# mLSTM numerators turned around, heads finished one by one, and the gate product moved ahead of the merge gates

## The reference, cut to what matters

```
proj = hn @ w_in                       # conv inputs, v, o, 16 gate columns, merge gates
s = einsum('bhcjd,bhcsd->bhcjs', qc, kc) * exp(dlog - m_j[..., None])
num = einsum('bhcjs,bhcsv->bhcjv', s, vc) + ...
den = sum(s, axis=-1) + ...
h = num / maximum(abs(den), exp(-m_j))[..., None]
y_b = o * (h_fwd + h_bwd)
mixed = sigmoid(merge_a) * (y_a @ w_branch_a) + sigmoid(merge_b) * (y_b @ w_branch_b)
```

## Time and profile before

| | |
|---|---|
| median of 3 runs | 2682.91 us (2682.42 to 2683.18) |
| the profiled execution | 2683.47 us, its span 2681.7 us |
| granted TensorE clock, mean | 0.993 of full |
| TensorE busy | 2626.6 us, 98% |
| VectorE busy | 1575.3 us, 59% |
| ScalarE busy | 1201.5 us, 45% |
| share of DMA engines' time | 50.2% for the weights |
| the load of a window, issue to landing | 5.9 us |

### The profile page before, as it was taken

How to read it: one execution, slowest core, us unless ns; L and a number is a source line. 1 busy time by engine, 2 the same in 40 slices (tenths; PEclk the granted TensorE clock), 3 DMA queues, 4 the chain that set the end, 5 groups by cost and what they waited for, 6 DMA issues and landing times.

```text
span 2681.7 us, 53183 instructions
## 1 busy us (share of the span) xinstructions
PE 2626.6 (98%) x21374; PEld 2541.4 (95%) x21374; DVE 1575.3 (59%) x1909; ACT 1201.5 (45%) x1402; POOL 43.1 (2%) x48
## 2 busy tenths in 40 slices
PE   8999999999999999999999988999999999999997
PEld 8999999999999989999999984679999999999997
DVE  6445778565465566777755454666565555555554
ACT  5444466443357654534444452124444444444432
POOL 0000121000000000000000000000000000000000
PEclk9999999999999999999999998999999999999999
DMA  6555532555545435656565550215655556565564
GB/s 223 178 175 169 168 102 80 165 177 175 178 159 171 134 103 165 198 191 197 194 202 193 191 180 16 71 63 188 194 191 190 188 188 199 185 202 195 191 193 130
DMA packets 123699, 445.95 MB, mean 166 GB/s; under 512 B 13594, under 2 KB 15925, under 8 KB 123440
## 3 DMA queue, kind: packets, MB, share of 16 engines
q1 hardware_dynamic: 122208, 438.82, 50.2%
q0 software_dynamic: 1360, 5.27, 0.6%
HBM read 441.94 MB, written 2.10 MB: 166 GB/s over the span
## 4 chain that ended last, share of the span: by engine, by line
PE 91%; DVE 4%; ACT 3%; issue 1%; DMA 0%; POOL 0%; DVEq 0%; SPq 0%; ACTq 0%
PE PS L1801 25%; PE PS L1799 25%; PE PS L1800 25%; PE PS L1862 2%; PE PS L1864 2%; PE PS L1863 2%; PE PS L2198 2%; PE PS L2266 1%; DVE lo L1025 1%; PE PS L2187 1%; ACT hi L530 1%; PE PS L1946 0%; PE PS L2209 0%; PE PS L1962 0%; PE PS L2045 0%
## 5 line engine op out<-in xcount | busy, mean ns | idle before, releaser
L1799 PE MATMUL PS<-XH,hi 128*128 128x256 f32 (+1 forms) x5152 | 1449.6, 281 | 15.7 <-DVE lo L1019 11.6
L1801 PE MATMUL PS<-XH,lo 128*128 128x256 f32 (+1 forms) x5152 | 1444.5, 280 | 0.0
L1800 PE MATMUL PS<-XL,hi 128*128 128x256 f32 (+1 forms) x5152 | 1440.0, 280 | 0.0
L1019 DVE TENSOR_TENSOR lo<-raw,hi 128x1024 fp32r<-128x1024 f32 x704 | 853.4, 1224 | 759.6 <-ACT hi L525 756.3
L525 ACT ACTIVATE hi<-raw 128x1024 fp32r<-128x1024 f32 x704 | 740.4, 1059 | 954.8 <-PE PS L1801 932.9
L1799 PEld LDWEIGHTS PS<-XH,hi 128*128 128x128 f32 x5152 | 969.6, 188 | 20.9 <-issue 19.2
L1800 PEld LDWEIGHTS PS<-XL,hi 128*128 128x128 f32 x5152 | 971.7, 189 | 2.3 <-issue 2.2
L1801 PEld LDWEIGHTS PS<-XH,lo 128*128 128x128 f32 x5152 | 969.2, 188 | 0.0
L1862 PE MATMUL PS<-XH,hi 128*128 128x256 f32 (+1 forms) x768 | 229.4, 299 | 0.3 <-DVE XL L1090 0.3
L1864 PE MATMUL PS<-XH,lo 128*128 128x256 f32 (+1 forms) x768 | 216.2, 282 | 0.0
L1863 PE MATMUL PS<-XL,hi 128*128 128x256 f32 (+1 forms) x768 | 216.0, 281 | 0.0
(11 more groups left out here) (327 smaller groups left out, 1598.9 us busy)
## 6 DMA issues: line engine op xcount, KB each, us to landing
raw<-stream SPq DMA_DIRECT2D x828, 512.0 KB, 4.1
H<-h_in SPq DMA_DIRECT2D x4, 544.0 KB, 8.3
y_win<-windows POOLq DMA_DIRECT2D x2, 1024.0 KB, 5.9
out<-H SPq DMA_DIRECT2D x4, 512.0 KB, 3.8
dftm<-dft POOLq DMA_DIRECT2D x1, 1024.0 KB, 5.9
w_t<-w POOLq DMA_DIRECT2D x2, 512.0 KB, 7.8
ml_m<-mask_ml POOLq DMA_DIRECT2D x1, 512.0 KB, 3.9
a_m<-masks_a POOLq DMA_DIRECT2D x1, 272.0 KB, 6.5
```

The lines of the kernel that those rows point to most:

```text
L1019: dve.tensor_tensor(halves(lo, s, q.tokens), raw_halves(s), halves(hi, s, q.tokens).bitcast(F32), ALU.subtract)\
L1799: pe.matmul(PS[:, bank, 0:n], w_hi, x_hi, start=start, stop=False)
L1800: pe.matmul(PS[:, bank, 0:n], w_hi, x_lo, start=False, stop=False)
L1801: return pe.matmul(PS[:, bank, 0:n], w_lo, x_hi, start=False, stop=stop)
```

## The change

Three things are changed together, with their places in SBUF.

1. **Order of the products.** `w2` is cut to 7 rounds. The mini product of the gates follows it, and then the merge gates as a product of their own, `mg`, of 4 rounds. The gate rows are made in between the chunks of `mg`'s first group; the extracts of both engines' lists are below. The stream of weights is in the new order.
2. **Numerators.** The weighted scores are now the stationary operand, the values the moving one, with a 257th column of ones. A numerator has the target tokens on partitions and its divisor in the last column. The matmuls of L2180 and L2280 are gone.
3. **Each head alone.** After each n VectorE makes two inverses for each partition (`divisors`); ScalarE scales the forward numerator (`forward`), VectorE scales the backward one and adds (`both_ways`), TensorE transposes the sum back (`m_turn`), and VectorE gates it (`mlstm_output`). The last head's end lies inside the first Hyena unit.

Beside these, the window buffer is one instead of two, its loads and that of the Fourier matrices are issued at other times, filter tiles of unit 0 go to banks 0, 1, 4 and 5, and the 16 `br_b` columns stand in other places: 0 and 1 before the first input spectrum, then (2, 3), (5, 6), (8, 9) and (11, 12, 13) ahead of the way back, (4), (7), (10) and (14, 15) behind it.

```
-    p["w2"] = Product(11, 8, 0, SEQ)
+    p["w2"] = Product(7, 8, 0, SEQ)
     p["gates"] = Mini(0, SEQ)
+    p["mg"] = Product(4, 8, 0, SEQ)
...
+            q = prod["mg"]                                       # ScalarE
+            tail_mg = follow(act, q, chunk, lambda: None, [(4, through(q, MG, 0, ACT.Sigmoid, "merge_gates"))],
+                             early={2: tail_w2, 4: gate_rows, 6: gate_logs}, nth=5)
...
+            q = prod["mg"]                                       # VectorE
+            tail_mg = follow(dve, q, chunk, lambda: None, [(4, scaled(q, MG, 0))],
+                             early={2: tail_w2, 3: mlstm_gates, 5: gate_sizes, 6: gate_sums, 7: gate_maxima})
...
+                def divisors(n):
+                    h, d = n // 2, n % 2
+                    dve.wait_ge(S("m_num"), n + 1)
+                    if n == 0:
+                        dve.wait_ge(S("m_c"), 2)
+                    r = m_R[:, n, :]
+                    den = PS[:, 4 + 2 * d:6 + 2 * d, 2 * P]
+                    own(dve.tensor_copy(r, den))
+                    own(dve.scalar_tensor_tensor(out=r, in0=r, scalar=-1.0, in1=r, op0=ALU.mult, op1=ALU.max))
+                    own(dve.tensor_tensor(r, r, m_F[:, 8 * d + h:8 * d + h + 5:4], ALU.max))
+                    own(dve.reciprocal(r, r), "m_r", n + 1)
...
+                for n in range(2 * MH + 2):
                     if n < 2 * MH:
...
+                        arguments(n)
+                    if n == 0:
+                        dve.memset(m_VT[:, :, :, 2 * P:2 * P + 1], 1.0).then_inc(S("m_ones"), 1)
+                    if n == 1:
+                        fill()
+                    if 1 <= n <= 2 * MH:
+                        weighted(n - 1)
+                    if n >= 2:
+                        divisors(n - 2)
+                        if n % 2 == 1:
+                            both_ways(n // 2 - 1)
+                            if n >= 5:
+                                mlstm_output(n // 2 - 2)
...
+            product(prod["mg"])
...
+            def m_numerators(n):
...
+                for tb in range(2):
                     for st in range(2):
-                        v = 2 * P * h + P * k
-                        ins = pe.matmul(PS[:, 4 + d, SEQ * k:SEQ * k + SEQ], m_VT[:, st, v:v + P], w[:, st, :],
+                        ins = pe.matmul(PS[:, 4 + 2 * d + tb, 0:2 * P + 1], w[:, st, 128 * tb:128 * tb + 128], m_VT[:, st, h, :],
                                         start=st == 0, stop=st == 1)
                 ins.then_inc(S("m_num"), 1)
...
             y_filters(0)
-            y_turn(0)
+            m_turn(MH - 1)
+            pe.wait_ge(S("dft_landed"), 16)
             y_filter_cosines(0)
...
+            pe.wait_ge(S("m_out"), MH)
+            y_turn(0)
             y_filter_sines(0)
-            m_divisors(2)
-            m_divisors(3)
+            branch_column(0)
             y_filters(1)
+            branch_column(1)
```

More of the change, by code:

```diff
@@ L1556, in mlstm_gates, with way, gate_sizes @@
                 dve.sem_inc(bank_free[0], 1)
-            def mlstm():
+            one = ones[0:MH, 0:1].to_broadcast([MH, SEQ])
+            def way(d, k):
+                return MR[:, 0, k, :] if d == 0 else MR[:, 1, k, ::-1]
+            def gate_sizes():
                 dve.wait_ge(S("m_gates"), 4)
@@ L1692, in branch_piece, with columns @@
                     lo_piece("branches", k, (MO if k < 2 else HY)[:, 4 * (k % 2):4 * (k % 2) + 4, :], SEQ)
+                def columns(fs):
+                    for f in fs:
+                        filled(f)
+                        ahead(f)
                 windowed(0)
-                mlstm_outputs()
-                windowed(1)
-                dve.wait_ge(S("y_uspec"), 1)
                 branch_piece(0)
                 branch_piece(1)
+                columns((0,))
+                windowed(1)
+                columns((1,))
                 for u in range(4):
@@ L1737, in _ @@
             q = prod["br_b"]
-            prep(q.c0)
-            prep(q.c0 + 1)
-            tail_w2()
-            prep(q.c0 + 2)
-            mlstm_gates()
-            prep(q.c0 + 3)
-            mixers()
+            for k in range(RING - 1):
+                prep(q.c0 + k)
+            tail_mg()
+            mlstm(lambda: prep(q.c0 + RING - 1))
+            hyena()
             tail2 = follow(dve, prod["br_a"], chunk, lambda: None, [(2, branch_a)], ready=RING)
@@ L2178, in _ @@
                 pe.wait_ge(S("m_p"), n + 1)
-                for st in range(2):
-                    pe.matmul(PS[0:16, 6 + d, 0:SEQ], one_hot(h), w[:, st, :], start=h == 0 and st == 0,
-                              stop=h == MH - 1 and st == 1)
-                if n >= 2:
-                    pe.wait_ge(S("m_nume"), n - 1)
-                for k in range(2):
+                if n == 0:
+                    pe.wait_ge(S("m_ones"), 1)
+                if n < 2:
+                    pe.wait_ge(S("m_v"), 4)
+                elif d == 0:
+                    pe.wait_ge(S("m_fw"), 2 * h)
+                else:
+                    pe.wait_ge(S("m_y"), 2 * h)
@@ new lines, in _ @@
+            pe.wait_ge(S("m_rows"), 1)
+            pe.wait_ge(bank_free[0], prod["br_a"].use0[0] + 1)
+            for row in range(2):
+                for d in range(2):
+                    for st in range(2):
+                        k = 16 * row + 8 * d + 4 * st
+                        ins = pe.transpose(PS[:, 3, k:k + 4], MR[:, d, row, 128 * st:128 * st + 128], ident[0:MH, 0:MH])
+            ins.then_inc(S("m_ct"), 1)
+            m_spread(0)
+            pe.wait_ge(bank_free[1], prod["br_a"].use0[1] + 1)
@@ new lines, in _ @@
+            for b in range(4):
+                for k in range(4):
+                    t = 4 * (b % 2) + k
+                    ins = pe.transpose(PS[:, 4 + b, 128 * k:128 * k + 128], MV[:, t, 128 * (b // 2):128 * (b // 2) + 128], ident)
+                ins.then_inc(S("m_vt"), 1)
+            pe.wait_ge(S("m_qk"), 4)
+            m_scores(0)
+            m_spread(1)
+            m_scores(1)
+            for n in range(2 * MH):
+                if n in (3, 5):
+                    m_scores(n // 2 + 1)
+                if n + 2 < 2 * MH:
+                    m_spread(n + 2)
+                m_numerators(n)
+                if n >= 3 and n % 2 == 1:
+                    m_turn(n // 2 - 1)
@@ L2309, in _ @@
                     y_filters(u + 2)
-                branch_column(4 * u + 3)
+                for f in columns_end[u]:
+                    branch_column(f)
             pe.wait_ge(S("y_out"), 4)
```

327 lines of the change are left out of this document (146 added, 181 removed).

## The result

Median 2660.95 us (2660.3 to 2662.74, 4 runs) against 2683.05 us of the kernel before on the same chip; the ratio is 0.9919, 95% interval 0.9907 to 0.9931. The profiled execution took 2660.54 us, span 2658.5. So the change is faster, by 22.1 us or 0.8%, where 29.7 us were forecast.

A forecast was written before the change was run, and what follows sets the result against it. TensorE was taken as the bound; -29.5 us up to the first input spectrum, -1.5 in it, -0.8 for a later wait and +2.06 at the merge product's opening gave -29.7, so 2653.2 us, range 2648 to 2661.

The forecast's parts named there:

- The columns in new places: Hyena units: moved `br_b` columns still cover the spectrum products; nothing counted, bounds -1 to +2 us.
- The other four window and filter operations are the same: Hyena units after the first input spectrum: remaining window and filter operations unchanged, so no cost counted.
- The rival of the clock: TensorE falls to 1.2 GHz again, as after 4.04 us idle: one fall 2656.2, two 2659.3; chance 0.28.
- the five waits that were listed: TensorE's waits from the merge product's opening to the first cosines: 2.06, 0.6, 0.25, 0.8 and 1.7 us.
- the opening: Start of `mg`: TensorE waits for VectorE to empty bank 0, filled by the mini product; cost +2.06 us.
- the divisor sums that went: mLSTM heads: eight divisor sums of 0.97 us each leave TensorE's work, 7.8 us.
- the 257th column for nothing: Numerator matmuls: 257 columns still take 1.92 us per n; far end +13.7 us, 2666.9, chance 0.02.
- the gate rows that just fit beside the ring: During `mg`: ScalarE and VectorE ready chunk 7's weights at 21.0 us, needed at 21.1; up to 0.5 late.
- the waits of 0.8 and 1.7 us: TensorE waits 0.8 us at the last two n of the heads, 1.7 us for window sums before the cosines.
- the stretch as a whole: From the end of `mg` to the first input spectrum: TensorE needs 56.75 us.
- The small operations of VectorE: Head loop: two-element operations taken as 0.16 us with 0.04 between; at 0.42 each, 8.3 us more, partly hidden.
- The rule on table loads: Gate rows beside `mg`: by the page's drain, the logarithm ends 2.8 us later, chunk 7 is 2.7 late; 2656.

The follow-up runs named there:

- cols12: The changed kernel with branch column 13 moved behind the way back of the last Hyena unit; 2655.36 us.
- fill11: The changed kernel with only VectorE's list altered: column 11 emptied before the last spectra product, TensorE's order untouched; 2658.03 us.
- filled_gap: The changed kernel with five unread 512-column matmuls filling TensorE's idle time between branch columns 12 and 13; 2658.32 us.
- den_sums: The changed kernel with 14 of the 16 removed divisor-sum matmuls put back, results unread; 2667.11 us.
- late_rows: The changed kernel with the gate rows made behind the merge product instead of beside its first group; 2674.67 us (7 runs).

## Why the prediction missed

- **What failed** is one step: "The columns in new places still cover the spectrum products: one column and four spectrum matmuls more or less on either side, and three columns in the last unit instead of two. Nothing for them, bounds -1 to +2." It asked what the columns cover and not what they wait for. Columns share two banks, so column f needs column f - 2 emptied; with three in a row, the third needs VectorE in the midst of its longest piece. In the profile that was 4.44 us of idle, and 2.9 us of clock with it, against bounds of -1 to +2 for the columns. cols12 and fill11 show the cause, filled_gap that the fall of the clock hangs on the idle. Before, two columns stood there, and TensorE waited at neither. A small miss of the same kind are the filters' waits for `y_K`, 0.6 us, where "The other four window and filter operations are the same" had nothing.
- **The rival of the clock** was right in kind: it did fall, though from a wait that was not foreseen. In the changed kernel's own profile it did not fall at the five waits that were listed; in cols12's profile it fell at two of them, the opening (1.8 us of idle) and the cosines (1.55 us, after 64-row filters). So "all are shorter than the 4.04 us" was no protection: falls came behind shorter ones, in some executions.
- **Right, with their sizes:** the divisor sums that went (0.97 us a pair, den_sums), the 257th column for nothing (1.93 against 1.92 us), the opening of `mg` (1.8 for 2.06), the gate rows that just fit beside the ring (0.2 us late at chunk 7, up to 0.5 allowed), the waits of 0.8 and 1.7 us (0.78 and 1.55) and the stretch as a whole, 55.42 for 56.75 us. The small operations of VectorE took 0.16 us with 0.03 between.
- **The rule on table loads:** the rows above have 0.01 us between a load's end and its activation, 0.02 between an activation and the next load. The drain of 1.38 us with each switch, in the Trainium skill's "ScalarE: Activation LUTs", section "What ACT_TABLE_LOAD costs", does not show in this trace, as the rows of before had said, and the 2656 worked out from it did not come about.
- **Other rivals:** VectorE did not set the pace of the heads (den_sums), and the rows were hidden (late_rows prices them at 13.7 us in the new order).
- **Where the range ended:** at 2661, which is 0.9918 of the kernel before; 0.9919 was measured, so the time lies at its very edge. That it comes so close is luck. The range went that far for falls of the clock at other places, for VectorE's pace and for rows left in the open, and the changed kernel's profile shows none of these; the columns' bound of +2, which bears on what did happen, was too narrow by more than 5 us.

## What to carry to other kernels

When work is moved as a cover for something else, list for each moved instruction what it waits for itself, the reuse of its PSUM banks above all, and where in the other engine's list the release stands. A wait that cannot be shortened can be postponed within the same work, as at both openings here: start with the banks that are free. A filler put in front of a consumer's input delays that consumer; look at who is bound behind it.

## What was not expected of the hardware

At the same place, behind the same instructions and the same idle time, the clock fell in some executions and not in others. Behind the 1.80 us at the opening of the merge product it fell in four of six profiles, behind the 1.55 us before the first cosines in six of nine, and behind the 4.44 us before column 13 in four of four. The cosines took 3.50 us in the changed kernel (1636.45 to 1639.95) and 5.05 to 5.21 us where the clock had fallen. In the head loop, where TensorE also waits 0.2 to 0.8 us at times and runs matmuls of four rows, it stayed at 2.4 GHz in the changed kernel's profile. Why one execution shows the fall and another does not was not found. For the reader this means that one profile cannot tell what a wait of this length costs, and that differences of one or two microseconds between whole times are at the edge of what four runs can show.
